# A two-layer fp32 trunk in split products: slots of the MLP's first and closing steps reordered, two gate blocks multiplied in turns, weight sums moved from VectorE to GpSimd

## The reference

```python
h = h + m                                  # the mixer's result
h = h + square(relu(rmsnorm(h) @ mlp_w1)) @ mlp_w2        # 2048 -> 8192 -> 2048
h = h + sigmoid(rmsnorm(h, norm_ple) @ ple_w_gate) * (p_i @ ple_w_proj)
```

## Time and profile before

| | |
|---|---|
| median of 3 runs | 2271.13 us (2269.78 to 2272.38) |
| the profiled execution, its own time | 2267.83 us |
| span of it, first to last instruction | 2266.1 us |
| mean granted TensorE clock | 0.995 |
| TensorE busy | 2215.4 us, 98% |
| VectorE busy | 1722.9 us, 76% |
| ScalarE busy | 1244.2 us, 55% |
| GpSimd busy | 157.0 us, 7% |

### The profile page before, as it was taken

One profiled execution on the slowest core, in us unless ns is written; L12 is line 12 of the kernel. 1 busy time (PEld: TensorE's weight loads), 2 busy tenths in 40 slices (PEclk: granted clock), 3 DMA queues, 4 the chain that ended last, 5 costly groups with the idle time before them and its releaser, 6 DMA issues.

```text
span 2266.1 us, 29676 instructions
## 1 busy us (share of the span) xinstructions
PE 2215.4 (98%) x10152; PEld 1837.0 (81%) x10152; DVE 1722.9 (76%) x1897; ACT 1244.2 (55%) x1542; POOL 157.0 (7%) x183
## 2 busy tenths in 40 slices
PE   8999999999999999988999999999999999999988
PEld 8998777888888888876888888878888888888766
DVE  6999868788788788666766667687877877876665
ACT  5666656556456556455644444555565565564554
POOL 3888000000000000000000000000000000000000
PEclk9999999999999999999999999999999999999999
DMA  9553598767767767597777777787677677685973
GB/s 343 161 165 134 170 297 247 233 207 242 226 206 241 227 200 240 163 272 237 220 247 216 219 240 219 255 243 223 215 237 220 217 233 224 210 237 152 288 250 111
DMA packets 499527, 503.53 MB, mean 222 GB/s; under 512 B 261041, under 2 KB 299121, under 8 KB 498417
## 3 DMA queue, kind: packets, MB, share of 16 engines
q1 hardware_dynamic: 497600, 499.71, 70.8%
q10 hardware_dynamic: 1696, 1.67, 0.2%
q0 software_dynamic: 144, 1.05, 0.1%
HBM read 464.62 MB, written 37.75 MB: 222 GB/s over the span
## 4 chain that ended last, share of the span: by engine, by line
PE 72%; DMA 5%; DVE 4%; SPq 2%; ACT 1%; issue 1%; DVEq 0%; ACTq 0%
PE acc L679 12%; PE acc L680 12%; PE acc L681 12%; PE acc L656 7%; PE acc L657 7%; PE acc L658 7%; PE tp L679 4%; PE tp L680 4%; PE tp L681 4%; DMA pT<-staged 2%; SPq L425 2%; DMA staged<-prows 1%; DMA pl<-in_mlp_w 1%; DVE wlo L1495 1%; DVE prows L1409 1%
## 5 line engine op out<-in xcount | busy, mean ns | idle before, releaser
L1495 DVE TENSOR_TENSOR wlo<-pl,whi 128x1024 fp32r<-128x1024 f32 x372 | 443.2, 1207 | 147.0 <-ACT whi L1011 141.3
L1011 ACT ACTIVATE whi<-pl 128x1024 fp32r<-128x1024 f32 x372 | 386.0, 1048 | 299.9 <-PE acc L681 195.7
L1325 DVE TENSOR_TENSOR wlo<-raw,whi 128x1024 fp32r<-128x1024 f32 x248 | 296.8, 1220 | 147.9 <-ACT whi L906 143.8
L906 ACT ACTIVATE whi<-raw 128x1024 fp32r<-128x1024 f32 x248 | 257.4, 1055 | 215.3 <-PE acc L658 215.1
L1011 ACT ACTIVATE whi<-raw 128x1024 fp32r<-128x1024 f32 x196 | 207.3, 1059 | 190.1 <-PE acc L681 127.5
L1495 DVE TENSOR_TENSOR wlo<-raw,whi 128x1024 fp32r<-128x1024 f32 x196 | 239.1, 1220 | 54.8 <-ACT whi L1011 51.1
L656 PE MATMUL acc<-whi,b_hi 128*128 128x512 f32 x672 | 263.5, 392 | 7.7 <-DVE b_lo L1429 4.8
L657 PE MATMUL acc<-wlo,b_hi 128*128 128x512 f32 x672 | 262.4, 391 | 0.0
L658 PE MATMUL acc<-whi,b_lo 128*128 128x512 f32 x672 | 262.4, 390 | 0.0
L679 PE MATMUL acc<-whi,a_hi 128*128 128x512 f32 x596 | 233.2, 391 | 5.7 <-DVE wlo L1495 5.6
L679 PE MATMUL acc<-whi,b_hi 128*128 128x512 f32 x596 | 232.6, 390 | 5.8 <-DVE wlo L1495 5.8
(11 more groups left out here) (218 smaller groups left out, 4045.5 us busy)
## 6 DMA issues: line engine op xcount, KB each, us to landing
pl<-in_mlp_w SPq DMA_DIRECT2D x368, 512.0 KB, 5.1
raw<-in_mlp_w SPq DMA_DIRECT2D x72, 1024.0 KB, 6.2
raw<-in_sc_w_in SPq DMA_DIRECT2D x48, 1024.0 KB, 5.7
raw<-in_cf_w_pw SPq DMA_DIRECT2D x64, 512.0 KB, 8.7
raw<-in_ple_w_gate SPq DMA_DIRECT2D x32, 1024.0 KB, 6.9
staged<-prows SPq DMA_DIRECT2D x240, 128.0 KB, 3.3
pT<-staged SPq DMA_DIRECT2D x56, 512.0 KB, 5.8
raw<-in_cf_w_pw SPq DMA_DIRECT2D x16, 1024.0 KB, 7.3
```

Of the source, the lines that this page charges most:

```text
L906: nc.scalar.activation(whi[:, e % SLOTS, :, :], raw[:, e // 2, 2 * (e % 2):2 * (e % 2) + 2, :], ACT.Copy).then_inc(hi_ready, 1)
L1011: nc.scalar.activation(whi[:, ring(parity, i), c, :], source[:, c, :], ACT.Copy).then_inc(slot_hi, 1)
L1325: nc.vector.tensor_tensor(wlo[:, e % SLOTS, :, :], raw[:, e // 2, 2 * (e % 2):2 * (e % 2) + 2, :], whi[:, e % SLOTS, :, :].bitcast(F32), A ...
L1495: nc.vector.tensor_tensor(wlo[:, ring(parity, i), c, :], source[:, c, :], whi[:, ring(parity, i), c, :].bitcast(F32), ALU.subtract).then_i ...
```

## The change

- FIRST takes m- and d-slots in alternation from its start, product 7 before 6 in part; HI1_FIRST goes from 13 to 10.
- END takes d20 and d21 before d02; the adds move from slots 15, 17, 21 to 17, 19, 21, the turns from 15, 18 to 17, 20, the operand of down block 0 from slot 19 to behind the last slot, HI1_END from 10 to 12; the gate's tiles are asked for at 6, 8, 10, 12.
- Gate blocks 0 and 1 are multiplied in turns, two halves of each (WOVEN, `multiply_woven`), so that operand block k is wanted after 4k halves. SP, ScalarE and VectorE have the gate's jobs in a new order.
- The eight weight sums of a step are issued by GpSimd (`weight_sums`), each waiting for VectorE's split of the slot that last used the field (`slot_lo`), for its own last sum and for the field's DMA. `weight_sum` of VectorE and `sums_after` go. VectorE's `mix` waits for `corners_done`, the later of m61 and m71.

```diff
@@ -38,15 +38,15 @@
-FIRST = (("m", 1, 0), ("m", 1, 1), ("m", 5, 0), ("m", 5, 1), ("d", 0, 0), ("m", 6, 0), ("d", 0, 1), ("m", 6, 1),
-         ("d", 1, 0), ("m", 7, 0), ("d", 1, 1), ("m", 7, 1), ("d", 0, 2), ("d", 0, 3), ("d", 1, 2), ("d", 1, 3)) + LATE
+FIRST = (("m", 1, 0), ("d", 0, 0), ("m", 1, 1), ("d", 0, 1), ("m", 5, 0), ("d", 1, 0), ("m", 5, 1), ("d", 1, 1),
+         ("m", 7, 0), ("m", 6, 0), ("d", 0, 2), ("m", 7, 1), ("d", 0, 3), ("m", 6, 1), ("d", 1, 2), ("d", 1, 3)) + LATE
 STEP = (("m", 1, 0), ("e", 3, 0), ("m", 1, 1), ("e", 3, 1), ("m", 5, 0), ("e", 3, 2), ("m", 5, 1), ("e", 3, 3),
         ("d", 0, 0), ("m", 6, 0), ("d", 0, 1), ("m", 6, 1), ("d", 0, 2), ("d", 0, 3),
         ("d", 1, 0), ("m", 7, 0), ("d", 1, 1), ("m", 7, 1), ("d", 1, 2), ("d", 1, 3)) + LATE
 END = (("e", 3, 0, None), ("e", 3, 1, None), ("e", 3, 2, None), ("e", 3, 3, None),
        ("d", 0, 0, None), ("d", 0, 1, None), ("d", 1, 0, 0), ("d", 1, 0, 1), ("d", 1, 1, 0), ("d", 1, 1, 1),
-       ("d", 0, 2, None), ("d", 0, 3, None), ("d", 1, 2, None), ("d", 1, 3, None),
-       ("d", 2, 0, None), ("d", 2, 1, None), ("d", 2, 2, None), ("d", 2, 3, None),
+       ("d", 2, 0, None), ("d", 2, 1, None), ("d", 0, 2, None), ("d", 0, 3, None), ("d", 1, 2, None), ("d", 1, 3, None),
+       ("d", 2, 2, None), ("d", 2, 3, None),
        ("d", 3, 0, None), ("d", 3, 1, None), ("d", 3, 2, None), ("d", 3, 3, None))
 STEPS = CHUNKS_UP - 1
@@ -58,8 +58,10 @@
 COMBO = {5: 0, 6: 1, 7: 2, 3: 3}
 BANK = {1: 0, 2: 0, 7: 1, 4: 1, 5: 2, 3: 2, 6: 3}
 IN_PLACE_AFTER = {5: 1, 6: 5, 7: None, 4: 6}
-OUT_ADD, OUT_TURN, OUT_SPLIT = (15, 17, 21), (15, 18), 19
-HI0, HI0_END, HIDDEN1, HI1, HI1_FIRST, HI1_END = 6, 4, 3, 12, 13, 10
+OUT_ADD, OUT_TURN = (17, 19, 21), (17, 20)
+GATE_LOADS = (6, 8, 10, 12)
+HI0, HI0_END, HIDDEN1, HI1, HI1_FIRST, HI1_END = 6, 4, 3, 12, 10, 12
+WOVEN = ((0, 0), (1, 0), (0, 1), (1, 1), (0, 2), (1, 2), (0, 3), (1, 3))
@@ -83,15 +85,13 @@
     def at(self, kind, of, part):
         return max(i for i, s in enumerate(self.slots) if s[:3] == (kind, of, part))
-    def sums_after(self, i):
-
-        out = []
-        for n in self.sums:
+    def sums_in_turn(self):
+
+        def when(n):
             _, of, part, _ = self.slots[n]
             user = IN_PLACE_AFTER[of]
-            if i == max(n - 3, 0 if user is None else self.at("m", user, part)):
-                out.append(n)
-        return out
+            return max(n - 3, 0 if user is None else self.at("m", user, part)), n
+        return sorted(self.sums, key=when)
...
     return t.at("m", 4, 1), t.at("m", 7, 1), t.at("m", 3, 1), t.at("m", 4, 1)
+def corners_done(t):
+    return max(t.at("m", 6, 1), t.at("m", 7, 1))
@@ -449,17 +453,41 @@
                     nc.sync.dma_start(xt, staged).then_inc(xt_ready, 16)
                 return back
+            def woven(w, n):
+
+                j, k = WOVEN[n]
+                return w[k * 4 * P:(k + 1) * 4 * P, cols(j)].rearrange("(c r) n -> r c n", r=P)
+
             def load_gate(layer):
-                unit, w, r3 = gate[layer], t_in["ple_w_gate"][layer], Result(mlp[layer][2], BLOCKS - 1)
+                unit, w, down = gate[layer], t_in["ple_w_gate"][layer], mlp[layer][2]
+                r1, r2, r3 = (Result(down, j) for j in (1, 2, 3))
+                take_back(r1)
+                if layer:
+                    sp.wait_ge(slot_used, first_slot(layer, STEPS))
+                    nc.sync.dma_start(gains[:, :], t_in["norm_final"].partition_broadcast(P)).then_inc(final_ready, 16)
+                stage_early(r2)
+                tile(unit.b + 1, 0, woven(w, 4))
+                tile(unit.b + 1, 1, woven(w, 5))
+                take_back(r2)
+                stage_early(r3)
+                tile(unit.b + 1, 2, woven(w, 6))
+                sp.wait_ge(slot_lo, freed(layer, STEPS, len(END) - 1))
+                if layer == 0:
+                    sp.wait_ge(emb_stored, 16 * 2 * BLOCKS)
+                nc.sync.dma_start(emb_in, emb_kept[:, layer, :, :]).then_inc(emb_back, 16)
+                tile(unit.b + 1, 3, woven(w, 7))
+                take_back(r3)
+                load(unit.b + 2, w, 2 * NB)
+                if layer:
+                    load(unit.b + 3, w, 3 * NB)
+                    return
                 for q in range(TILES):
-                    tile(unit.b + 1, q, w[q * 4 * P:(q + 1) * 4 * P, NB:2 * NB].rearrange("(c r) n -> r c n", r=P))
-                    if q == 0:
-                        stage_early(r3)
-                    if q == 1:
-                        take_back(r3)
-                with sp.Fori(2, BLOCKS) as j:
-                    load(unit.b + j, w, j * NB, back=exchange(Result(unit, j - 2)))
+                    if q in (0, 3):
+                        stage_early(Result(unit, q // 2))
+                    tile(unit.b + 3, q, w[q * 4 * P:(q + 1) * 4 * P, 3 * NB:4 * NB].rearrange("(c r) n -> r c n", r=P))
+                    if q in (1, 3):
+                        take_back(Result(unit, q // 2))
             def keep_emb(i):
@@ -554,8 +582,7 @@
                 def gate_tile(q):
                     if q == 0:
                         sp.wait_ge(slot_lo, freed(layer, STEPS - 1, max(field_freed(STEP))))
-                    nc.sync.dma_start(raw[:, q, :, :], gate_w_in[q * 4 * P:(q + 1) * 4 * P, 0:NB]
-                                      .rearrange("(c r) n -> r c n", r=P)).then_inc(raw_ready[q], 16)
+                    nc.sync.dma_start(raw[:, q, :, :], woven(gate_w_in, q)).then_inc(raw_ready[q], 16)
                 for i in range(len(t)):
...
                         take_back(c1)
-                    if i in (8, 10, 12, 18):
-                        gate_tile((8, 10, 12, 18).index(i))
+                    if i in GATE_LOADS:
+                        gate_tile(GATE_LOADS.index(i))
                     for j in range(2):
                         if i == OUT_TURN[j] - 1:
                             stage_early(Result(down, j))
-                        if i == OUT_TURN[j] + j:
-                            take_back(Result(down, j))
-                if layer:
-                    sp.wait_ge(slot_used, first_slot(layer, STEPS))
-                    nc.sync.dma_start(gains[:, :], t_in["norm_final"].partition_broadcast(P)).then_inc(final_ready, 16)
-                stage_early(Result(down, 2))
-                sp.wait_ge(slot_lo, freed(layer, STEPS, len(t) - 1))
-                if layer == 0:
-                    sp.wait_ge(emb_stored, 16 * 2 * BLOCKS)
-                nc.sync.dma_start(emb_in, emb_kept[:, layer, :, :]).then_inc(emb_back, 16)
-                take_back(Result(down, 2))
+                    if i == OUT_TURN[0]:
+                        take_back(Result(down, 0))
             def stage_product(j):
...
                     multiply(unit.b + j, unit.a + j, j % 2, xin)
+
+            def multiply_woven(unit, xin, ready):
+
+                for n, (j, k) in enumerate(WOVEN):
+                    if k == 0:
+                        pe.wait_ge(acc_free, unit.a + j - BLOCKS + 2)
+                    for i in range(2):
+                        e, p = 2 * k + i, 2 * n + i
+                        pe.wait_ge(operand_ready, ready + e + 1)
+                        half(unit.b + p // HALVES, p % HALVES, j, *xin, (2 * e, 2 * e + 1), e == 0, e == HALVES - 1)
@@ -856,7 +884,9 @@
             multiply_unit(pw2, X[1], (y_ready, 0))
             multiply_mlp(0, 0, (operand_ready, 2 * pw2.o))
-            multiply_unit(gate[0], X[0], (operand_ready, 2 * mlp[0][2].o))
+            multiply_woven(gate[0], X[0], 2 * mlp[0][2].o)
+            for j in (2, 3):
+                multiply(gate[0].b + j, gate[0].a + j, j % 2, X[0])
             multiply(win.b, win.a, 0, X[1], (operand_ready, 2 * gate[0].o))
...
@@ -941,7 +970,7 @@
                     first = 2 if r.kind == "gate" else 2 + BLOCKS
                     if r.j == 0:
                         nc.scalar.activation(table[:, first:first + 1], ident[:, 0:1], ACT.Sigmoid)
-                    act.wait_ge(half_used, HALVES * r.b + HALVES)
+                    act.wait_ge(half_used, HALVES * r.b + (HALVES if r.j else 2 * HALVES - 2))
                     act.wait_ge(acc_free, r.a)
                     act.wait_ge(res_ready, r.t)
...
@@ -1052,8 +1081,6 @@
                         if i == (HI1_END if end else HI1):
                             operand_hi(before[1].x, 2 * parity + 1, hid)
                     if end:
-                        if i == OUT_SPLIT:
-                            operand_hi(Result(down, 0).x, 0, X[u], gain)
                         for j in range(3):
                             if i == OUT_ADD[j]:
                                 keep(Result(down, j))
@@ -1065,6 +1092,8 @@
                             hidden(Result(chunk(layer, k), 0), up_free)
                     slot_split(layer, k, parity, i, product_source(t, n, i) if kind == "m" else
                                plain_source(layer, k, t.load[i]), single)
+                if end:
```

(71 more changed lines are left out.)

68 lines of the change are left out of this document (44 added, 24 removed).

## The result

The changed kernel takes **2381.18 us** (median of 4 runs, 2377.77 to 2384.45) against 2271.76 for the kernel before: ratio 1.048, interval 1.0466 to 1.0493. I had forecast 2256, within 2240 to 2290, with 0.24 for slower.

The account below looks back on a forecast made before the run. TensorE, busy 98% of 2266.1 us, was the bound, so only idle time could be won. Gate 13.8 + closing step 2.0 + first step 1.0 - sums 2.0 = 14.8 gave 2253.0, as a median 2256, range 2240 to 2290.

Parts of the forecast that it names:

- near misses: MLP loop: charge of 2.0 us over 12 steps for GpSimd's sums holding VectorE up; bounds a gain of nothing, loss of 78.
- rows 11 and 12: Trace rows read as GpSimd and VectorE's two-input split excluding each other, VectorE getting in between two GpSimd operations.
- rival A: From 454.7 to 486 of later steps, GpSimd takes a turn between any two splits: 79 us lost, 2333; chance 0.18.
- Seen from the average: 77.1 of 84.4: Loop step: VectorE's 67.6 us less 9.7 for the sums plus GpSimd's 19.2 gives 77.1 of the step's 84.4.
- Rival B: One sum per step gets in at the tight place, 1.3 us x 12 = 16: 2270, no change; chance 0.16.
- A sum on GpSimd: A 1024-wide sum on GpSimd takes 2.4 us, half way between 1.76 and 2.95.
- The first step: First MLP step with m- and d-slots interleaved: gain of 1.0 us for both layers together, bounds -5 to +8.
- The gate and the closing step: Gate blocks in turns gain 13.8 us; the closing step's new order gains 2.0, 1.0 in each layer.
- at nothing: Gate: SP issues the same tiles in another order, asked for 14 us ahead, so no cost; one late tile 3.3 us.
- my 6 us to spare: Gate: fourth operand ready at 1051 and wanted about 1058, so no idle time and no fall of the clock.
- Rival C: The order wins little, late down weights or gate halves: 5 of 16.8 us remain, less 2: 2268; chance 0.08.
- The clock: Forecast: 1.0 throughout; a rival had first-step idle time pulling it down, 2 us in each layer, inside the range.

Follow-up runs that it names:

- pool_paced: The changed kernel with each GpSimd weight sum held until the third slot before its own, instead of issued as early as data allow: 2293.66 us, ratio 1.0094.
- order_only: The changed kernel with its eight weight sums per step back on VectorE, the new order kept: 2267.97 us, ratio 0.9989 to the kernel before.
- pool_two: The changed order with two of each step's eight sums (those of product 4) on GpSimd, the other six on VectorE: 2270.95 us, ratio 0.9993.
- pool_writes: The changed kernel with GpSimd's subtraction replaced by a memset of the same output, weight sums left out of the result: 2267.99 us, ratio 0.9987.
- order_old_first: The changed kernel with sums on VectorE and the first step's old table and HI1_FIRST at 13: 2271.36 us, ratio 1.0003.
- all_four: Changed order, sums on VectorE; gains' wait moved later, keep behind the high split, take_back(r3) earlier, layer 0's gate block 1 operand behind the sixth split: 2237.98 us.

## Why the prediction was wrong, by its own steps

- **The step that failed** is "I charge **2.0** over 12 steps for near misses", which rests on "If GpSimd gets in only where VectorE idles, a split is at most 2.4 late" and on the reading of rows 11 and 12 that GpSimd waited to the very end. What it stood for measured 99 us over the 12 steps and 11 more in the two first ones. GpSimd gets in between any two splits: its row starts at 471.72, during a split of VectorE's, and the next split, which follows with no gap, takes 3.4 us and ends behind the sum. That the two exclude each other over the whole instruction I had right; who wins a tie I took from one pair of rows (VectorE between two GpSimd instructions) as if it held only in that direction.
- The Trainium skill, "SBUF — State Buffer", section on who interferes with whom, says that a VectorE instruction with two SBUF inputs contends with a GpSimd instruction that reads SBUF, not with one that only writes it; that the contention is an exclusive lock; and, in its item on VectorE's two-port modes, that whoever issues first has the shared pair for the whole instruction. The runs agree, and show the last for these two-input splits too: a split takes 1219 ns beside a memset, 2.1 us where it meets a copy, 3.4 us where it meets a sum. Applied to a waiting GpSimd instruction and a VectorE whose next one can only issue when the last is over, it gives alternation. By it rival A deserved more than 0.18.
- **"Seen from the average: 77.1 of 84.4"** was true and no argument: the sums do fit into the step, but issued as early as their data allow, all eight stand between 454.6 and 489.5, six of them from 466 on, and from 454.7 to 486 VectorE had 1.7 us to spare in 31.3. pool_paced shows what spacing them is worth: 88 us.
- **Rival A** was the mechanism, with its place. Its 79 us for the 12 steps match the 79 of stalls there, in part by luck: it set VectorE's and GpSimd's work against the length of the stretch, and pool_paced, with six sums in much the same place, loses only 1.3 per step. The 48 us between its 2333 and the measured 2381 are the lower clock behind the stalls (20), the two first steps (20.2 against 7.6 in order_only, 13) and the gain of 16.8 that it counted on, of which order_only shows some 2.5 (14). The range ended at 2290. **Rival B** (one sum in a step at the tight place) was not what happened, eight stood there; what one alone costs there no run shows, pool_two's two stand behind it.
- **The prize was nothing.** The forecast gave the sums a bound of "a gain of nothing", and pool_writes shows that this was the best case: 117 us of work taken from VectorE won no time.
- **A sum on GpSimd** takes 2.40 us alone; I took 2.4.
- **The first step**: 1.0 taken, 3.4 measured, inside its bounds.
- **The gate and the closing step**: 15.8 us of gain taken, none measured (order_old_first, 1.0003). Part of the mechanism held: no wait for operand parts, and the three adds at 5.95. In layer 1 of order_only the gate itself lost 4.4 us where it had lost 9.2, but the closing step 14.5 where it had lost 8.5: the load of the gains had moved behind another entry of the queue. I costed SP's reordering "at nothing" and did not list that DMA, nor who waits for it. In layer 0 the fourth operand was back 12.8 us after it was asked for and not the 6.28 of rows 9; my 6 us to spare were used up by 3 MB of loads (emb's 2 and a gate tile's 1) ahead of it. And I stopped at the blocks that were woven: the same lateness came back at the last block (6.5). With these waits and the `keep` out of the way the new order is 33 us ahead of the kernel before; what the same edits bring in the old order was not tried, so how much of the 33 belongs to the reorder stays open.
- **Rival C** (the order wins little, 5 of 16.8) is what that half did: 0.9989, about 2.5 us. Its reasons were others (late down weights, late halves); the waits for the gains and for the read-back were not among them.
- **The clock** was not 1.0 throughout: the lower level came once in eleven of the twelve later steps, at the longest stall, as in the window above. In the twelfth (1671 to 1686) it stayed at 1.0 behind a stall just as long.

## What to carry to other kernels

Before work leaves an engine, ask what its absence would win: here it was nothing. Before work goes to GpSimd, ask whether its instruction reads SBUF while VectorE runs instructions with two SBUF inputs, and then count on strict alternation: each VectorE instruction of a back-to-back row gets longer by one whole GpSimd instruction. That was free where TensorE had splits in hand and costly where such delays followed one another and each split took longer than TensorE's slot, so set their places and cut them short, and don't judge by busy sums. When the order of a queue changes, list every DMA that moved and look for the in-order engine that waits for it: three such waits (6.6, 4.1 and 5.6 us) stood against what the new order should have won.

## What the runs showed of the hardware

- A GpSimd subtraction of 128x1024 float32 takes 2.40 us alone, a copy 1.0, a memset 0.96; beside splits 3.3, 1.9 to 2.0 and still 0.96.
- A VectorE addition with one input in PSUM takes 1.21 us beside a GpSimd sum (482.73), where splits with both inputs in SBUF take 3.4.
- More time taken from VectorE (202 us against 156) went with less time lost (85.7 against 174.6).
- At stalls of 2.8 us of TensorE the clock fell to the lower level in eleven of twelve steps (0.69 in the mean from 486 to 497) and stayed up in one, while a stall of 1.7 us left the stretch from 470 to 486 at 1.00. With the stalls gone the clock comes back: mean 0.981 in the changed kernel, 0.998 in all_four.
